# Attention values with high and low halves in one weight tile, and the softmax scale moved to GpSimd, in an fp32 encoder kernel

## The reference, cut to what matters

```
s = (einsum('bqhd,bkhd->bhqk', qn, k_nope) + einsum('bqhr,bkr->bhqk', qp, k_pe))
p = softmax(s * scale, axis=-1)          # 512 queries x 512 keys, per head
o = einsum('bhqk,bkhd->bqhd', p, v)      # value width 64
```

## Time and profile before

| | us |
|---|---|
| median of 3 runs | 1542.7 (1542.68 to 1542.95) |
| the profiled execution, its own time | 1543.31 |
| its span, first to last instruction | 1541.5 |
| PE busy, share of the span | 1464.7, 95% |
| DVE busy, share | 774.7, 50% |
| ACT busy, share | 686.9, 45% |
| POOL busy, share | 660.2, 43% |
| mean granted TensorE clock | 0.990 |

### The profile page before, as it was taken

The page is one execution under the profiler, slowest core; times in us unless marked ns, Lnnn a source line. Parts: engine busy times, 40 slices in busy tenths (PEclk is TensorE's granted clock), DMA queues, the critical chain, the costliest instruction groups (busy, mean ns, idle before and its releaser), DMA issues.

```text
span 1541.5 us, 19395 instructions
## 1 busy us (share of the span) xinstructions
PE 1464.7 (95%) x6838; PEld 1194.5 (77%) x6838; DVE 774.7 (50%) x1188; ACT 686.9 (45%) x1084; POOL 660.2 (43%) x317
## 2 busy tenths in 40 slices
PE   4998889999999999999999898999999999999994
PEld 4776669888878888888878565898888888888883
DVE  5738768633454530345164876792526445024443
ACT  4566636444343431344355664563534444124441
POOL 4443226743344444343545321585343444434440
PEclk9999999999999999999999999999999999999997
DMA  5320114521233243322423101354122332323221
GB/s 171 121 84 15 41 55 137 178 82 42 82 96 98 81 122 96 93 82 86 126 83 107 44 28 55 96 175 127 38 86 68 110 101 80 119 82 109 84 67 55
DMA packets 39032, 138.74 MB, mean 90 GB/s; under 512 B 4848, under 2 KB 5104, under 8 KB 38704
## 3 DMA queue, kind: packets, MB, share of 16 engines
q1 hardware_dynamic: 37440, 134.23, 28.4%
q10 hardware_dynamic: 1520, 3.52, 0.7%
HBM read 135.64 MB, written 2.10 MB: 89 GB/s over the span
## 4 chain that ended last, share of the span: by engine, by line
PE 78%; issue 10%; DVE 7%; POOL 4%; ACT 1%; POOLq 0%; DVEq 0%; ACTq 0%
PE ps L1284 25%; PE ps L1286 25%; PE ps L1285 25%; POOL w_lo L340 4%; PE ps L1436 1%; DVE small L988 1%; DVE h_lo L1014 1%; PE ps L1294 1%; DVE work L1091 0%; DVE small L1018 0%; DVE arena L1014 0%; PE ps L1459 0%; DVE work L1000 0%; DVE work L1074 0%; DVE arena L1164 0%
## 5 line engine op out<-in xcount | busy, mean ns | idle before, releaser
L340 POOL TENSOR_TENSOR w_lo<-raw,w_hi 128x1024 fp32r<-128x1024 f32 x248 | 605.0, 2457 | 721.0 <-ACT w_hi L436 720.8
L1284 PE MATMUL ps<-h_hi,w_hi 128*128 128x512 f32 (+1 forms) x1040 | 407.9, 392 | 26.0 <-POOL w_lo L340 20.5
L1285 PE MATMUL ps<-h_lo,w_hi 128*128 128x512 f32 (+1 forms) x1040 | 403.9, 388 | 0.0
L1286 PE MATMUL ps<-h_hi,w_lo 128*128 128x512 f32 (+1 forms) x1040 | 403.9, 388 | 0.0
L436 ACT ACTIVATE w_hi<-raw 128x1024 fp32r<-128x1024 f32 x248 | 255.8, 1054 | 326.6 <-PE ps L1286 326.5
L1284 PEld LDWEIGHTS ps<-h_hi,w_hi 128*128 128x128 f32 x1040 | 195.9, 188 | 69.3 <-issue 28.8
L1284 PE MATMUL ps<-arena,w_hi 128*128 128x512 f32 (+2 forms) x656 | 244.1, 372 | 0.9 <-DVE arena L970 0.9
L1286 PE MATMUL ps<-arena,w_lo 128*128 128x512 f32 (+2 forms) x656 | 241.9, 369 | 0.0
L1285 PE MATMUL ps<-arena,w_hi 128*128 128x512 f32 (+2 forms) x656 | 241.8, 369 | 0.0
L1285 PEld LDWEIGHTS ps<-h_lo,w_hi 128*128 128x128 f32 x1040 | 195.9, 188 | 40.8 <-issue 1.0
L1286 PEld LDWEIGHTS ps<-h_hi,w_lo 128*128 128x128 f32 x1040 | 195.8, 188 | 40.2
(11 more groups left out here) (169 smaller groups left out, 1793.5 us busy)
## 6 DMA issues: line engine op xcount, KB each, us to landing
raw<-blocks_d SPq DMA_DIRECT2D x248, 512.0 KB, 3.5
x<-xT_d SPq DMA_DIRECT2D x4, 512.0 KB, 7.7
work<-memT_d ACTq DMA_DIRECT2D x2, 1024.0 KB, 4.9
outT_d<-work SPq DMA_DIRECT2D x8, 256.0 KB, 2.2
work<-ln_d ACTq DMA_DIRECT2D x2, 512.0 KB, 3.6
par<-par_d ACTq DMA_DIRECT2D x2, 113.5 KB, 2.8
work<-pos_d ACTq DMA_DIRECT2D x1, 128.0 KB, 6.4
mix_g<-par_d ACTq DMA_DIRECT2D x2, 4.0 KB, 6.3
```

What stands on the lines that cost most here:

```text
L340: gp.tensor_tensor(w_lo[:, b % SPLIT, :], raw[:, b % RAW, :], w_hi[:, b % SPLIT, :].bitcast(F32), ALU.subtract).then_inc(lo_done.sem, 1)
L1284: pe.matmul(out, a_hi, b_hi, start=first, stop=False)
L1285: pe.matmul(out, a_hi, b_lo, start=False, stop=False)
L1286: return pe.matmul(out, a_lo, b_hi, start=False, stop=last)
```

## The change

1. The high and the low part of a head's values (64 columns each) lie side by side in `v_pair`, so that one 128-column weight tile holds both. `attend` issues for each of four key tiles one matmul with that tile and the high probabilities (result on 128 partitions of bank 5: high product below, low product above) and one with the high values and the low probabilities: 8 matmuls a head, not 12.
2. `copy_sums` becomes `copy_part`: ACT copies partitions 64 to 127 of bank 5, at t = 2 behind `attend`, and `attended` adds it.
3. `spread_sums` and its transposes are gone. Instead GpSimd multiplies the exponentials with the reciprocal (`prob`, 128x512, in place), before `turn(i)`, which now waits for it. DVE takes each column's reciprocal by itself (`recip_sum(i+2)`, at the end of step i).
4. GpSimd's order is written out by steps: `prob(i+2)` in each, `low` and `query_low` behind it, `gate_low` at `LOW_STEPS`.

```diff
+LOW_STEPS = ((1, 3), (2, 1), (2, 3), (3, 3))
...
-        v_hi, v_lo = arena[:, 8:12, :], arena[:, 12:16, :]
+        v_pair = arena[:, 8:16, :].rearrange("p (k a) n -> p k (a n)", k=TT).rearrange("p k (h s d) -> p k h s d", s=2, d=VD)
+        v_hi, v_lo = v_pair[:, :, :, 0, :], v_pair[:, :, :, 1, :]
...
+                def prob(i):
+                    need(hrec_done, i + 1)
+                    gp.tensor_tensor(e[:, i % 3, :], e[:, i % 3, :],
+                                     hrec[:, i % 8:i % 8 + 1].to_broadcast([P, SEQ]), ALU.mult)\
+                        .then_inc(prob_done.sem, 1)
+
-                for b in range(B_V + AHEAD, B_V + 7):
+                for b in range(B_V + AHEAD, B_V + 6):
                     low(b)
+                prob(0)
+                prob(1)
+                low(B_V + 6)
                 for h in range(HEADS):
-                    if h % 2 == 1:
-                        low(B_V + 7 + h // 2)
-                    if h + 2 < HEADS:
-                        query_low(h + 2)
-                        if h in (2, 3):
-                            gate_low(2 * h - 4)
-                            gate_low(2 * h - 3)
+                    for t in range(TT):
+                        i = TT * h + t
+                        if (h, t) in LOW_STEPS:
+                            gate_low(LOW_STEPS.index((h, t)))
+                        if i + 2 < HEADS * TT:
+                            prob(i + 2)
+                        if t == 0 and h % 2 == 1:
+                            low(B_V + 7 + h // 2)
+                        if t == 1 and h + 2 < HEADS:
+                            query_low(h + 2)
...
-                def copy_sums(h):
-                    need(spread, h + 1)
+                def copy_part(h):
+                    need(pv_mm, h + 1)
                     if h > 0:
                         need(o_done, h)
-                    act.activation(rsum, ps[3][0:64, :], ACT.Copy).then_inc(rsum_done.sem, 1)
+                    act.activation(part, ps[5][64:128, :], ACT.Copy).then_inc(part_done.sem, 1)
...
-                def recip_sums(h):
-                    need(exp_done, TT * h + TT)
-                    c = slice(4 * (h % 2), 4 * (h % 2) + 4)
+                def recip_sum(i):
+                    need(exp_done, i + 1)
+                    c = slice(i % 8, i % 8 + 1)
                     dve.reciprocal(hrec[:, c], hsum[:, c]).then_inc(hrec_done.sem, 1)
...
                 def turn(i):
-                    need(exp_done, i + 1)
+                    need(prob_done, i + 1)
...
                     for k in ks:
-                        last = product3(ps[5][0:VD, :], v_hi[:, k, c], v_lo[:, k, c],
-                                        pt_hi[h % 2][:, k, :], pt_lo[h % 2][:, k, :], k == 0, k == TT - 1)
+                        both = v_pair[:, k, h, :, :].rearrange("p s d -> p (s d)")
+                        if k < TT - 1:
+                            pe.matmul(ps[5][:, :], both, pt_hi[h % 2][:, k, :], start=k == 0, stop=False)
+                        pe.matmul(ps[5][0:VD, :], v_hi[:, k, h, :], pt_lo[h % 2][:, k, :], start=False, stop=False)
+                        if k == TT - 1:
+                            last = pe.matmul(ps[5][:, :], both, pt_hi[h % 2][:, k, :], start=False, stop=True)
...
-                def spread_sums(h):
...
-                    if t == 0 and h >= 1:
-                        spread_sums(h - 1)
```

More of the change, by code:

```diff
@@ L179, in encoder_program @@
         rs_tok = small[:, 60:64]
-        rsum = work[0:64, 11, :]
+        part = work[0:64, 11, :]
         hsum, hrec = small[:, 80:88], small[:, 88:96]
@@ L520, in layer @@
                         block_used(B_WV)
-                    act.activation(v_hi[:, t, :], ps[BB[t]][:, :], ACT.Copy).then_inc(vh_done.sem, 1)
+                    act.activation(v_hi[:, t], ps[BB[t]][:, :].rearrange("p (h d) -> p h d", d=VD), ACT.Copy)\
+                        .then_inc(vh_done.sem, 1)
                 for t in range(TT):
@@ L606, in layer @@
                         square_output(SQUARE_STEPS.index((h, t)))
-                    if t == 1 and h >= 1:
-                        copy_sums(h - 1)
+                    if t == 2 and h >= 1:
+                        copy_part(h - 1)
                     if t == 2 and h + 2 < HEADS:
@@ L625, in layer @@
                 gate_turned(2)
-                copy_sums(HEADS - 1)
+                copy_part(HEADS - 1)
                 square_output(3)
@@ L1046, in layer @@
                 amax(2)
+                recip_sum(0)
+                recip_sum(1)
                 for i in range(HEADS * TT):
@@ L1095, in layer @@
                     turned_lo(i)
-                    if t == 3:
-                        recip_sums(h)
+                    if i + 2 < HEADS * TT:
+                        recip_sum(i + 2)
                 gate_turned(2)
@@ L1444, in attend @@
                             need(o_done, h)
-                    c = slice(VD * h, VD * h + VD)
                     for k in ks:
-                        last = product3(ps[5][0:VD, :], v_hi[:, k, c], v_lo[:, k, c],
-                                        pt_hi[h % 2][:, k, :], pt_lo[h % 2][:, k, :], k == 0, k == TT - 1)
+                        both = v_pair[:, k, h, :, :].rearrange("p s d -> p (s d)")
[4 more added lines that the diff above has]
+                            last = pe.matmul(ps[5][:, :], both, pt_hi[h % 2][:, k, :], start=False, stop=True)
                     if ks[-1] == TT - 1:
                         last.then_inc(pv_mm.sem, 1)
-                def spread_sums(h):
-                    need(hrec_done, h + 1)
-                    if h > 0:
-                        need(rsum_done, h)
-                    for t in range(TT):
-                        c = 4 * (h % 2) + t
-                        last = pe.transpose(ps[3][:, P * t:P * t + P], hrec[:, c:c + 1].to_broadcast([P, P]), ident[:, :])
-                    last.then_inc(spread.sem, 1)
                 def mix(n):
@@ L1518, in layer @@
                 attend(HEADS - 1)
-                spread_sums(HEADS - 1)
                 def mixed(k):
```

16 lines of the change are left out of this document (8 added, 8 removed).

## The result

| | before | change |
|---|---|---|
| median, us | 1542.69 (1539.79 to 1542.95, 4 runs) | 1552.7 (1550.48 to 1553.21, 4 runs) |
| ratio, 95% | | 1.007 [1.0058, 1.0082] |
| span of the profiled execution, us | 1541.5 | 1550.9 |
| mean granted clock | 0.990 | 0.979 |

A forecast was written before the change was run, and what follows sets the result against it. PE bounds the whole kernel; in the attention loops DVE is near full too, fuller in the first 45 us. Per layer 8.5 - 1.7 + 0.4 + 1.6 - 2.15 = +6.65, two layers +13.3: 1542.7 to 1556.0 us, range 1536 to 1566.

The forecast's parts named there:

- Term 1: Loop start: `recip_sum(0)` behind `amax(2)` delays `turn(0)` from 103.49 to 105.2, so PE and DVE start +1.7 us later.
- Term 2: Step (1, 1): DVE's small SBUF steps stall under `prob(6)` and `low`, 2.4 us lost against 1.0 now: +1.4.
- Term 3: Step (1, 3): the layer norm on DVE meets POOL's queue, two stalls of 0.85 + 0.7, now none: +1.5.
- Term 4: Single reciprocals on DVE: three more a head at 0.09 us, nine while DVE is full: +0.8.
- Term 5: Step (3, 1): `low` again before the layer norm, 2.1 us, where `query_low` costs 1.0 now: +1.1.
- Term 6: `mix(0)`: `gate_low(3)` queued on POOL behind `prob` and `query_low`; 6.1 us behind `turned_lo(13)`, now 3.5: +2.6.
- The credit of 0.6: Ahead of `mix(0)`: head 1's `attend` and projections are partly PE's, so its saving gives -0.6 us.
- The recovery behind `mix(0)`: Heads 3 to 5, where PE's share is highest: about 1.7 us of their 3.8 come back.
- The tail: Last head of each layer, at the lower clock with nothing beside it: 4 x 0.43 + 0.44 = 2.15 us saved.
- The rule of the shared ports: POOL's instruction blocks DVE steps with two SBUF inputs or a two-port mode; so `prob` blocks too, keeping +13.
- the third rival: Clock falls too: one more 6 us stretch at 1.2 GHz behind `mix(0)`, +2.8 a layer, 1561.6 us; chance 0.15.
- PE's saving lands: Rival, faster: POOL's multiplications are hidden and about 7.5 of 10.2 us a layer land, -5 a layer, 1532.7; chance 0.20.

The follow-up runs named there:

- GpSimd's order: Changed kernel with GpSimd's block subtractions moved to other steps and the last `gate_low` ahead of `query_low(5)`: 1543.61 us, ratio 1.0011.
- The run with three matmuls: Changed kernel with three matmuls a value tile again (12 a head), no `copy_part`, `attended` a copy out of PSUM: 1561.87 us, ratio 1.0134.
- the fillers: Changed kernel with unused matmuls on PE, 12 before `turn(7)`, 10 ahead of `mix(0)`, 6 before `turn(30)`: 1550.19 us, ratio 1.0055.
- both orders: Changed kernel with the first two reciprocals ahead of `amax(2)` and GpSimd's block subtractions moved to other steps: 1538.84 us, ratio 0.9976.
- the multiplication aside: Changed kernel with GpSimd's multiplications on other data into an unread buffer, each awaiting the previous; turns don't wait, scaling left out: 1548.43 us, ratio 1.0048.

## Why the prediction was right, and where its sizes were off

- **Sign and place: right.** It is slower because stalls and late turns take more than PE's cut gives, mostly in the first 50 us of the loop. The experiments bear out both causes: without the multiplication -24 us, with GpSimd's order -9.1, with the reciprocals moved -10.9.
- **The price of `prob`: too high.** 1.045 us, not 1.25, and under the lower bound of 1.2 that I took from twice L380. It is a term of every place where several stand in a row. I leaned towards L358, which has two full inputs; the row with the same operands was nearer.
- **Term 1** (+1.7): 1.4 us at `turn(0)`, as its `prob` is 0.2 shorter. Removing it gave 4.5 us for both layers instead of 2.9.
- **Term 2** (+1.4): right. L918 loses 2.24 us, before 1.0 was lost at L1074: +1.2.
- **Term 3** (+1.5): right. Two held steps, (0.85 - 0.55) + (1.65 - 0.69) = 1.3.
- **Term 4** (+0.8): right. The reciprocals stand 0.08 us ahead of what follows (116.98 to 117.06).
- **Term 5** (+1.1): too large. L1089 loses 1.34 (1.89 against 0.55) at step (3, 1), against 1.0 lost there before: +0.35. I had let DVE reach the step early in `low`; it came 0.8 us into it.
- **Term 6** (+2.6): too large, +1.9. `mix(0)` starts 5.5 us behind `turned_lo(13)`, before 3.5, predicted 6.1; the chain of `prob`, `query_low`, `prob`, `gate_low` from 148.11 on is there as written, each `prob` shorter.
- **The credit of 0.6** for PE's own saving ahead of `mix(0)`: too small. The measured terms make 1.4 + 1.2 + 1.3 + 0.8 + 0.35 + 1.9 = 7.0, and the timeline is 5.6 behind: 1.4 was given back. The run with three matmuls says the same for the whole kernel: two thirds of that saving land.
- **The recovery behind `mix(0)`** (-1.7): at `turn(25)` the change is 3.2 behind, so -2.4. By `turn(31)` it is 5.8 behind: +2.6 where I had 0.4 + 1.6. The three held steps that I named are there with 0.4 to 0.5 us each, not 0.7, so they don't explain it. Most of it, 1.5 us, comes between `turn(27)` and `turn(28)`, where the scores wait for an exponential that ACT issues behind `copy_part` and a block's high part (184.98 to 186.52):

```profile
187.38 0.50 PE L1301 MATMUL ps<-arena 128*128 128x512 f32 x1 [1.45 <-ACT work L559]
```

Another 1.0 comes between `turn(30)` and `turn(31)`, where the matmuls of `attend` stand 0.43 us apart. The forecast had neither in its sum: `copy_part` stood there at nothing, with 0.6 us a head should its cover go.

- **The tail** (-2.15): right in layer 0, half in layer 1. From `turn_gated(2)` to the first projection it was 6.34 us (196.30 to 202.64) and is 4.33 (200.90 to 205.23): -2.0. In layer 1 it was only 5.34 (945.49 to 950.83), as the last three of the twelve matmuls stood 0.23 us apart there, and is 4.33 again: -1.0. The forecast took both layers for alike. Its 0.44 us for `spread_sums` in the tail are in no row; the trace before has 0.35 (202.29 to 202.64).
- **The rule of the shared ports: right.** L1023 and L918 are held under `prob` alone, and steps with an input in PSUM (0.67 to 0.69 us), the reciprocals (0.14 to 0.16) and the batch statistics (0.68) keep their times in the change. The Trainium skill, "SBUF — State Buffer", section "SBUF: two separate sides", gives two SBUF inputs of DVE, against a GpSimd instruction that reads SBUF, as a case that blocks; the rows agree, even for 4 elements a partition (2.39 us for 0.15). The held scaling of before, L1091 at 186.96, which the forecast leaned on, stands under this `low` (before), whose row it did not show:

```profile
186.43 2.38 POOL L340 TENSOR_TENSOR w_lo<-raw,w_hi 128x1024 fp32r<-128x1024 f32 x1 [1.33 <-ACT w_hi L436]
```

- **The clock: in part.** It fell in more places than the forecast took (0.94 and 0.75), as the third rival said. What the fillers restored was worth about 2 us, not the 5.6 on top of the forecast that it gave; the end of the loop is untested.
- **The signs named ahead.** Seen: `turn(0)` 1.9 us behind the start of `amax(2)` (101.78 to 103.71; 2.3 said), L918 at 2.39 us, L1091 and L1089 over 1 us, `mix(0)` 5.5 us behind `turned_lo(13)`. PE's wait at `mix(0)` is 2.9 us, under the 3 to 4 said. Turns wait for `prob` in heads 1, 2 and 6 as said, once in head 3, and also in heads 0 and 7, which was not. PE's busy time fell by 7.0 us, not some 20.

Against the 10.6 us of the loops, the sum of +13.3 was 2.7 too high. Up to `mix(0)` the errors went one way, 8.5 for 5.6, by the length of `prob` and too little credit for PE. Behind it they went both ways: more recovery, a worse end of the loop, half the tail in layer 1. That these cancel in part is luck. "PE's saving lands" was no wrong mechanism but the other half of the same balance: it prevails with the first reciprocals ahead, `low` elsewhere, and the multiplications 0.6 us earlier.

**How the 24 us of the multiplication divide.** These kernels issue the same 1236 instructions on DVE, so its busy time, over that without the multiplication, is an estimate of how long the multiplications held DVE steps (whole program, us; with both orders `low` stands elsewhere too):

| kernel | DVE busy | held | PE's waits for `prob` | ratio |
|---|---|---|---|---|
| without the multiplication | 770.7 | | | 0.9913 |
| the multiplication aside | 786.5 | 15.8 | none | 1.0048 |
| the change | 781.9 | 11.2 | 28.9 | 1.007 |
| the change, reciprocal earlier | 776.6 | 5.9 | 19.0 | 0.9999 |
| both orders, reciprocal earlier | 774.0 | 3.3 | 10.0 | 0.9928 |
| both orders, reciprocal behind `amax` | 780.9 | 10.2 | 1.0 | 0.997 |

In the last row the turns hardly wait for `prob`; against the row above it DVE is held 6.9 us longer, and the kernel is 6.5 us slower. With the multiplication aside, 15.8 us held and 4.6 more of waiting at the two `mix(0)` (8.0 for 3.4) make 20.4 of the 21 us that remain. If held time counts nearly whole, as these two pairs suggest, about 11 of the change's 24 us are held steps. That is an estimate from sums, not a run.

**What stays open.** How the other 13 us divide between waiting turns, the late `mix(0)` and the low clock. Held steps and waiting turns feed each other (a held DVE makes the next reciprocal late), and no run here takes one away alone. Nor did I try to do the multiplication on ACT, or the `low` parts elsewhere.

## What to carry to other kernels

Work given to an idle GpSimd is not free when VectorE is near full: price it by which VectorE steps with all inputs in SBUF stand under it, and place it under steps that read PSUM. When a new stage sits between two engines, look at its place in the producer's queue as well as at its length: one line here was worth 11 us, about as much as taking 64 matmuls away (9.9). Try each side of such a trade alone before judging it; the change was slower as written and is 0.7% faster than the kernel before with three small moves.

## What the runs showed that I had not expected

- GpSimd multiplies 128x512 by a column in 1.045 us, against 1.27 for a subtraction of two full inputs of the same shape with fp32r output, a fifth less. Whether the broadcast input, the operation or the output type saves it, no run parts.
- A DVE instruction of 4 elements a partition can be held for 2.24 us; size is no protection.
- With the shorter `attend(7)` the clock comes back later against the work: in layer 0 the first projections behind it start 0.43 us apart (205.23 to 205.66), where before they were 0.23 apart (202.96 to 203.19). That takes back 0.6 us of the tail's gain, 3.8 to 4.4 us behind. In layer 1 it is 0.75 of 1.0: most of what that layer loses more is its smaller tail.
- Earlier is not always better: reciprocals at the end of the step, before the last subtraction, and behind `amax` gave 0.9976, 0.9928 and 0.997 with the same GpSimd order.
